# Attention of a one-core transformer step: keys on partitions, probabilities as the stationary operand, a ones column for the denominators

## What is computed

```python
def block_attention(q, k, v):
    ...
    def one_block(qblk):
        s = jnp.einsum('bkgqd,bskd->bkgqs', qblk, k).astype(jnp.float32) * scale
        p = jax.nn.softmax(s, axis=-1).astype(v.dtype)
        return jnp.einsum('bkgqs,bskd->bkgqd', p, v)
```

## Time and profile before

| | us |
|---|---|
| median of 3 runs | 3546.38 (3546.01 to 3548.62) |
| the profiled execution | 3547.59 |
| its span in the profile | 3545.8 |
| attention, from its first to its last DMA issue | 705.6 to 1744.7 |
| TensorE busy, whole span | 3171.3 (89%) |

### The profile page before, as it was taken

How to read it: one execution, slowest core, us unless ns; L and a number is a source line. 1 busy time by engine, 2 the same in 40 slices (tenths; PEclk the granted TensorE clock), 3 DMA queues, 4 the chain that set the end, 5 groups by cost and what they waited for, 6 DMA issues and landing times. The chain is left out here.

```text
span 3545.8 us, 60756 instructions
## 1 busy us (share of the span) xinstructions
PE 3171.3 (89%) x21856; PEld 2900.2 (82%) x21856; DVE 1878.6 (53%) x3485; ACT 1671.7 (47%) x3239; POOL 388.6 (11%) x400
## 2 busy tenths in 40 slices
PE   6999994759999999999699756999999999999991
PEld 6788883748888888888588645999999999999991
DVE  2222226548888888888533365545455445545443
ACT  2222220547777777777434202455455544455442
POOL 0333333500000000000000000010010000110001
PEclk9999997869999999999799855999999999999996
DMA  5121113410000000000244204565565555665545
GB/s 217 43 80 60 67 66 116 140 42 25 27 27 27 27 27 27 27 27 27 81 147 150 83 0 132 174 192 185 179 198 184 183 187 179 188 193 181 181 130 220
DMA packets 307599, 393.69 MB, mean 111 GB/s; under 512 B 13808, under 2 KB 263872, under 8 KB 306496
## 3 DMA queue, kind: packets, MB, share of 16 engines
q1 hardware_dynamic: 293680, 338.64, 28.9%
q0 software_dynamic: 10240, 35.66, 4.4%
q10 hardware_dynamic: 3600, 18.35, 1.3%
HBM read 318.68 MB, written 74.06 MB: 111 GB/s over the span
## 5 line engine op out<-in xcount | busy, mean ns | idle before, releaser
L2304 DVE TENSOR_TENSOR e_w_lo<-e_raw,e_w_hi 128x2048 fp32r<-128x2048 f32 x192 | 440.1, 2292 | 490.4 <-ACT e_w_hi L2246 490.4
L92 PE MATMUL e_ps<-e_x_hi,e_w_hi 128*128 128x272 f32 x2048 | 602.1, 294 | 5.5 <-issue 5.5
L94 PE MATMUL e_ps<-e_x_hi,e_w_lo 128*128 128x272 f32 x2048 | 593.8, 290 | 0.0
L93 PE MATMUL e_ps<-e_x_lo,e_w_hi 128*128 128x272 f32 x2048 | 590.1, 288 | 0.0
L2246 ACT ACTIVATE e_w_hi<-e_raw 128x2048 fp32r<-128x2048 f32 x192 | 366.1, 1907 | 163.7 <-DMA e_raw<-in_w_gate 159.3
L1470 DVE TENSOR_TENSOR a_pT_lo<-a_ps_t,a_pT_hi 128x512 fp32r<-128x512 f32 (+1 forms) x648 | 368.0, 601 | 139.5 <-ACT a_pT_hi L1368 139.2
L1368 ACT ACTIVATE a_pT_hi<-a_ps_t 128x512 fp32r<-128x512 f32 (+1 forms) x648 | 319.6, 532 | 185.1 <-PE a_ps_t L1238 180.5
L92 PEld LDWEIGHTS e_ps<-e_x_hi,e_w_hi 128*128 128x128 f32 x2048 | 386.1, 189 | 7.1 <-issue 5.5
L93 PEld LDWEIGHTS e_ps<-e_x_lo,e_w_hi 128*128 128x128 f32 x2048 | 386.9, 189 | 0.0
L94 PEld LDWEIGHTS e_ps<-e_x_hi,e_w_lo 128*128 128x128 f32 x2048 | 385.8, 188 | 0.0
L1443 DVE TENSOR_REDUCE a_mx<-a_ps_s 128x1 f32<-128x896 f32 (+2 forms) x392 | 346.1, 890 | 26.8 <-PE a_ps_s L1228 26.8
(11 more groups left out here) (269 smaller groups left out, 5478.2 us busy)
## 6 DMA issues: line engine op xcount, KB each, us to landing
e_raw<-in_w_gate SPq DMA_DIRECT2D x64, 1024.0 KB, 5.2
e_raw<-in_w_up SPq DMA_DIRECT2D x64, 1024.0 KB, 5.2
e_raw<-in_w_down SPq DMA_DIRECT2D x64, 1024.0 KB, 5.2
a_wm<-in_w_mod SPq DMA_DIRECT2D x32, 512.0 KB, 4.0
s_ret<-p_pr SPq DMA_DIRECT2D x17, 768.0 KB, 3.6
m_raw<-in_w_in ACTq DMA_DIRECT2D x8, 1152.0 KB, 7.1
o_cT<-s_ct SPq DMA_DIRECT2D x17, 512.0 KB, 4.7
s_x<-o_x SPq DMA_DIRECT2D x17, 512.0 KB, 4.9
```

What stands on the lines that cost most here:

```text
L92: nc.tensor.matmul(out, w_hi, x_hi, start=first, stop=False)
L93: nc.tensor.matmul(out, w_hi, x_lo, start=False, stop=False)
L94: return nc.tensor.matmul(out, w_lo, x_hi, start=False, stop=last)
L2304: nc.vector.tensor_tensor(w_lo[n % RING][:, :, :], raw[n % RING][:, :, :], w_hi[n % RING][:, :, :].bitcast(F32), ALU.subtract).then_inc(w_ ...
```

## The change

The key tile moves to the partitions of the scores. A slot is one query tile `i` and one key head `v`, thus 4 query heads side by side, 512 columns (`QCOLS`).

- Scores (L1249, L1250): a key tile is stationary, 512 query columns move; a second matmul adds the low key part. The softmax's maximum must be subtracted by matmul now, since queries are no longer on partitions: row 64 of `a_keys_lo` holds ones and row 64 of `a_qM` the negated maxima. The exponential (L1389) leaves probabilities that are transposed already.
- The maxima come from rough scores (L1222, L1218), high key part only, computed one slot ahead in the old layout: 17 pieces, 16 of 512 columns and one of four times 128, through two banks `a_ps_r`. DVE reduces each (L1496, L1493), takes the maximum of all (L1507), TensorE transposes it (L1231), ACT stores it negated.
- High and low parts are made from SBUF, two key tiles (1024 columns) at a time: `high` (ACT, L1401), `low` (DVE, L1514), 9 pairs per slot, the last with one tile.
- Value product (L1265, L1267): probabilities are stationary, per key tile and head one matmul with the high part against [ones, value high, value low], 130 columns, and one with the low part against [ones, value high], 66 columns. Column 0 of the result is the denominator, so the sums of the exponential, their reduction and the folding matmuls go. ACT copies the result out (L1410), DVE takes the reciprocal (L1530), POOL adds the halves and divides.
- The key pass keeps tile i-1 after it has rounded tile i. The load of the first queries goes ahead of it.
- Each engine walks `slot`, with 9 steps `j`; TensorE multiplies values two steps behind the scores.

```diff
+PAIRS = (KEY_TILES + 1) // 2
+QCOLS = QPK * P
+PARTS = (KEY_TILES - 1) * P // QCOLS
+PIECES = PARTS * QPK + 1
+PIECES_IN = [2, 2, 2, 2, 2, 2, 2, 3, 0]
+ONES = 2
+VCOLS = ONES + 2 * HD
+QUADS = NKV * NT
+RING = 3
...
-        prob = [k.sb(f"a_prob{i}", [P, KEY_TILES * P]) for i in range(2)]
-        pT_hi = [k.sb(f"a_pT_hi{i}", [P, KEY_TILES, GROUP, P], F32R) for i in range(2)]
-        pT_lo = [k.sb(f"a_pT_lo{i}", [P, KEY_TILES, GROUP, P], F32R) for i in range(2)]
...
+        prob = k.sb("a_prob", [P, RING, 2, QCOLS])
+        p_hi = k.sb("a_p_hi", [P, PAIRS, 2, QCOLS], F32R)
+        p_lo = k.sb("a_p_lo", [P, PAIRS, 2, QCOLS], F32R)
+        o_all = k.sb("a_o_all", [P, QPK, VCOLS])
...
+        ps_m = k.ps("a_ps_m", [P, QCOLS])
+        ps_r = [k.ps(f"a_ps_r{i}", [P, 512]) for i in range(2)]
+        ps_s = [k.ps(f"a_ps_s{i}", [P, QCOLS]) for i in range(3)]
+        ps_o = [k.ps(f"a_ps_o{i}", [P, 512]) for i in range(2)]
...
+            def combine(i, v):
+                n = quad(i, v)
+                pool.wait_ge(o_kept, 2 * n + 2)
+                nc.gpsimd.tensor_tensor(o_sum[:, :, :], o_all[:, :, ONES:ONES + HD], o_all[:, :, ONES + HD:VCOLS], ALU.add).then_inc(added, 1)
+                pool.wait_ge(added, n + 1)
+                pool.wait_ge(rsum_ok, n + 1)
+                nc.gpsimd.tensor_tensor(att[:, QPK * v:QPK * (v + 1), :], o_sum[:, :, :], spread(rsum[:, :], [P, QPK, HD]),
+                                        ALU.mult).then_inc(att_ok, 1)
...
+            def rough(i, v, n):
+                if n == 0:
+                    pe.wait_ge(emptied, use_of_queries(i, v) + 1)
+                if not (first_slot(i, v) and n < 2):
+                    pe.wait_ge(max_ok, piece(i, v, n) - 1)
+                to = ps_r[piece_bank(i, v, n)]
+                if rest_of_keys(i, n):
+                    src = (CTX_KEYS if ctx_tile(i) else KEY_TILES - 1) * P
+                    for c in range(QPK):
+                        ins = nc.tensor.matmul(to[:, c * P:(c + 1) * P], qT[v][:, c * P:(c + 1) * P], keys[:, v, src:src + P],
+                                               start=True, stop=True)
+                else:
+                    c, part = n // PARTS, n % PARTS
+                    ins = nc.tensor.matmul(to[:, :], qT[v][:, c * P:(c + 1) * P], keys[:, v, part * QCOLS:(part + 1) * QCOLS],
+                                           start=True, stop=True)
+                ins.then_inc(rough_ok, 1)
+            def turn_top(i, v):
+                pe.wait_ge(top_ok, quad(i, v) + 1)
+                pe.wait_ge(emptied, use_of_top(i, v))
+                for c in range(QPK):
+                    ins = nc.tensor.transpose(ps_m[0:HD + 1, c * P:(c + 1) * P], top[:, c, :], g["ident"][:, :])
+                ins.then_inc(filled, 1)
+            def scores(i, v, j, t):
+                c = 2 * j + t
+                n = key_tile_of(i, v, c)
+                to = ps_s[bank(i, v, c)]
+                if c == 0:
+                    pe.wait_ge(emptied, use_of_top(i, v) + 1)
+                    pe.wait_ge(qM_ok, quad(i, v) + 1)
...
+                src = CTX_KEYS if ctx_tile(i) else c
+                nc.tensor.matmul(to[:, :], keys[:, v, src * P:(src + 1) * P], qT[v][:, :], start=True, stop=False)
+                nc.tensor.matmul(to[:, :], keys_lo[:, v, src * P:(src + 1) * P], qM[v][:, :], start=False, stop=True)\
+                    .then_inc(scored, 1)
+            def value(i, v, j, t):
+                n = pair(i, v, j)
+                if t == 0:
+                    pe.wait_ge(hi_ok, n + 1)
+                    pe.wait_ge(lo_ok, n + 1)
+                    if j == 0 and not first_slot(i, v):
+                        pe.wait_ge(o_kept, 2 * quad(i, v))
...
+                for c in range(QPK):
+                    q = slice(c * P, (c + 1) * P)
+                    nc.tensor.matmul(out_block(c), p_hi[:, place(i, v, j), t, q], vals[:, src, v, :],
+                                     start=first and c in (0, 3), stop=False, skip_group_check=True)
+                    ins = nc.tensor.matmul(out_block(c)[:, 0:ONES + HD], p_lo[:, place(i, v, j), t, q], vals[:, src, v, 0:ONES + HD],
+                                           start=False, stop=last, skip_group_check=True)
+                if t == tiles_of(i, j)[-1]:
                     ins.then_inc(valued, 1)
...
+            def slot(i, v):
+                last, ahead = before(i, v), following(i, v)
+                at = 0
+                for j in range(PAIRS):
+                    todo = list(range(at, min(at + PIECES_IN[j], pieces_of(ahead[0]))))
+                    at = at + PIECES_IN[j]
+                    if j == 0:
+                        if not first_slot(i, v):
+                            for t in range(2):
+                                value(*last, PAIRS - 2, t)
+                        turn_queries(*ahead)
+                    for t in tiles_of(i, j):
+                        scores(i, v, j, t)
+                        if todo and j and t == 0:
+                            rough(*ahead, todo.pop(0))
+                    if j == PAIRS - 1:
+                        turn_top(*ahead)
+                    if j == 1 and not first_slot(i, v):
+                        value(*last, PAIRS - 1, 0)
+                    for t in range(2):
+                        if j >= 2:
+                            value(i, v, j - 2, t)
+                        if todo:
+                            rough(*ahead, todo.pop(0))
+                    if j == 2:
+                        modulation(i, v)
+                    if j == 5 and not first_slot(i, v):
+                        turn_out(*last)
...
+            def keep_keys(i, j):
                 act.wait_ge(k_turned, i + 1)
-                out = keys[:, :, :, i * P:(i + 1) * P] if isinstance(i, int) else keys[:, :, :, bass.ds(i * P, P)]
-                nc.scalar.activation(out.rearrange("p n v t -> p (n v) t"), ps_t[j][:, :, :], ACT.Copy).then_inc(k_kept, 1)
-            over_pairs(act, key_tile, 2, NTA // 2, 0)
+                at = slice(i * P, (i + 1) * P) if isinstance(i, int) else bass.ds(i * P, P)
+                nc.scalar.activation(keys[:, :, at], ps_s[j][:, 0:2 * P].rearrange("p (v t) -> p v t", t=P), ACT.Copy)\
+                    .then_inc(k_kept, 1)
+                nc.scalar.activation(keys_lo[0:HD, :, at], ps_s[j][0:HD, 2 * P:4 * P].rearrange("p (v t) -> p v t", t=P),
+                                     ACT.Copy).then_inc(k_kept, 1)
+            def key_tile(h, off):
+                round_keys(h, off)
+                if not known(h, off, 0):
+                    keep_keys(2 * h + off - 1, (off - 1) % 2)
...
+            def exps(i, v, j, t):
+                c = 2 * j + t
+                act.wait_ge(scored, key_tile_of(i, v, c) + 1)
+                if t == 0 and not (first_slot(i, v) and j < RING):
+                    act.wait_ge(lo_ok, PAIRS * (QUADS - 1) + 7 + v if ctx_tile(i) else pair(i, v, j) - RING + 1)
+                nc.scalar.activation(prob[:, place(i, v, j) % RING, t, :], ps_s[bank(i, v, c)][:, :], ACT.Exp, scale=scale)\
+                    .then_inc(exped, 1)
+            def high(i, v, j):
+                n = pair(i, v, j)
+                m = len(tiles_of(i, j))
+                act.wait_ge(exped, key_tile_of(i, v, 2 * j) + m)
...
+                nc.scalar.activation(p_hi[:, place(i, v, j), 0:m, :], prob[:, place(i, v, j) % RING, 0:m, :], ACT.Copy)\
+                    .then_inc(hi_ok, 1)
+            def keep_sums(i, v):
+                act.wait_ge(valued, pair(i, v, 0) + (1 if ctx_tile(i) else PAIRS))
+                if not first_slot(i, v):
+                    act.wait_ge(att_ok, quad(i, v))
+                for b, lo, hi in ((0, 0, 3), (1, 3, QPK)):
+                    nc.scalar.activation(o_all[:, lo:hi, :], ps_o[b][:, 0:(hi - lo) * VCOLS].rearrange("p (h f) -> p h f", f=VCOLS),
+                                         ACT.Copy).then_inc(o_kept, 1)
...
+            def slot(i, v):
+                last, ahead = before(i, v), following(i, v)
+                for j in range(PAIRS):
+                    if j == 0:
+                        keep_queries(*ahead)
+                    if j == 2 and not first_slot(i, v):
+                        keep_sums(*last)
+                    if j == 6 and not first_slot(i, v):
+                        keep_out(*last)
+                    for t in tiles_of(i, j):
+                        exps(i, v, j, t)
+                    if j == PAIRS - 1:
+                        keep_top(*ahead)
+                    high(i, v, j)
+                    if j == 2 and v == 0:
+                        queries_hi(i + 1)
...
+            def copy_queries(i, v):
+                dve.wait_ge(emptied, use_of_queries(i, v) + 1)
+                nc.vector.tensor_copy(qM[v][0:HD, :], qT[v][0:HD, :].bitcast(F32)).then_inc(qM_ok, 1)
+            def maxima(i, v, n):
+                dve.wait_ge(rough_ok, piece(i, v, n) + 1)
+                src = ps_r[piece_bank(i, v, n)]
```

(37 more changed lines are left out.)

608 lines of the change are left out of this document (235 added, 373 removed).

## The result

The changed kernel takes 4243.21 us (median of 4, 4241.84 to 4249.41), the kernel before 3547.2 on the same chip: ratio 1.197, 95% interval 1.194 to 1.199. It is slower, as forecast, but by 696 us and not by 45, far outside the range.

What follows compares the result with a forecast made beforehand. TensorE was taken as the bound: 32 slots of 32.1 us from 755 us, with corrections at the first and last, reach 1776; with the context tile 1790 against 1744.7. That is +45 on 3547.6: 3593 us, range 3520 to 3662.

Steps and rivals of the forecast that it cites:

- Price of a matmul: TensorE in attention: each narrow value product with new weights costs 0.112 us, whether 130 or 66 columns.
- that rival: Value products in attention: narrow matmuls cheaper, 0.085 us each, saving 117 us, so 3476 us; chance 5%.
- Together 30.0, so 60.0 for a tile: TensorE's work in attention: 30.0 us a slot, 60.0 a query tile, against 53.5 before.
- plus 2 for its half clock: First attention slot: 2 us added because TensorE runs it at half clock.
- 32.1: Each attention slot: 30.0 us of TensorE work plus 2.1 us of waits.
- Waits: TensorE, each slot: 1.37 us at its end, 0.23 for rough(2), 0.51 for the last slot's sums; together 2.1.
- The hand-over: Between engines, such as DVE's subtraction to TensorE's transposes: 0.03 to 0.05 us each.
- Key pass: Before the attention slots: 1.8 us a key tile against 2.87, keys ready at 741 us instead of 760.
- the 14 us for the start: Between key pass and first scores: query transposes, 17 pieces at DVE's 0.59, maxima, transposes; scores start at 755 us.
- Sign: Whole kernel: slower than before, given 76%; faster 18%, within 0.2% 6%.
- the wait at the slot's end: Step 7 to 8: value(6) waits 1.37 us for DVE's low(6), queued behind the last pieces and the maximum of all.

Runs made afterwards that it cites:

- the first row of plain matmuls: Changed kernel plus plain matmuls on TensorE alone behind attention's context tile (512 columns, pairs of 130 and 66, 130 alone, 256, two mixes); 4652.28 us, one run.
- the second row: Changed kernel plus plain matmuls behind attention's last tile: slot-like steps of 512s and pairs of 130 and 66, run behind 512s, 2-column matmuls or pairs; 4894.85 us, one run.

## Why the prediction was wrong

- **Price of a matmul: right.** 0.11 us for a product of 130 or 66 columns at the full clock, as in the earlier trace rows; 60.0 us of work for a tile, measured 60.5 where nothing waits. The Trainium skill, page "TensorE: Matmul & The Clock Gate", section "Back-to-back issue gap", has about 81 ns for each pair of a weight load and a 128-column matmul; the traces here disagree, the 130-column products alone ran 0.112 apart (2593 to 2626 us of the first row of plain matmuls), so that rival was rightly small.
- **The clock: the step that failed.** "Together 30.0, so 60.0 for a tile" was priced by rows at the full clock only, and the prediction carried this clock of the old stage over to a new mix, with "plus 2 for its half clock" as the only exception. The order put two stretches poor in wide matmuls into every slot; at a granted 0.57 the work of 30.0 us takes 30.0/0.57 = 53, measured 51.8. 32 x (51.8 - 32.1) = 630 of the missing 650 us. The rows of before could not have told: at 0.50 in the key pass and 0.63 in the context tile TensorE was also idle for much of the time (busy for 21.9 of 59.0 and 19.3 of 28.0 us). That a stage can be busy throughout and slow is new here: 277.8 of 280 us busy at 0.57. The Trainium skill, page "TensorE: Matmul & The Clock Gate", section "What's actually happening", says that activity releases the throttle; if activity is read as busy time, this trace disagrees. Neither the range nor a rival of the prediction allowed for a half clock.
- **Waits.** In the changed kernel nearly gone, since ScalarE and VectorE keep their pace while TensorE is slow (0.21 us before the transposes of the maxima at 1527.06, TensorE idle for 2.2 of 280 us). At the full clock, with the 256-column products, 1.16, 0 and 0.21 against 1.37, 0.23 and 0.51: 0.7 a slot too much, 24 us. The hand-over that the prediction put at 0.03 to 0.05 us is 0.06 in the row it names, which changes none of this.
- **Key pass: right, the start behind it too short.** The key tiles were rounded 1.83 us apart (708.1 to 739.2 us, 17 periods), forecast 1.8. First scores came at 761.3 us, forecast 755, before 764.2: of the 14 us for the start, the 16 first pieces were counted at VectorE's 0.59 each, but at the half clock TensorE set their pace, 0.79 (743.95 to 756.57).
- **Sign: luck.** Slower for the reason given would have been an estimated 3590 us (3550 without the wait at the slot's end, and 32 x 1.2) to 3620 (3653 with 256 columns, less 35 for the width); the sign of the real result was right by another mechanism.

Still open: what property of a matmul counts, and how the mix around a burst enters. Width and memory together go far: 130 columns alone held the full clock in the row and did not raise it from half, and low products of 130 gave 0.65 with the burst in place, 0.89 without it. But 130 with 66 fell in the row where 130 alone did not. And a burst can bring the clock down in wide surroundings too (nine times in the kernel before with 128 and 128, twice and three times in the two kernels with 512 columns of probabilities moving), where it is back 3.4 us later and not 41 to 48; in the kernel before and among products of 256 there was no such fall. Why some bursts do it and others don't is not shown.

## What to carry to other kernels

Before pricing a new mix of matmuls at the full clock, look for stretches of a few us without wide ones, and spread these (transposes, 2-column products, narrow value products) between wide matmuls; reordering left every count and width as it was and was worth 696 us here. Such an order keeps a full clock; it need not bring one: the steps of the second row, at the full clock for 58 us, stayed at half for 111 us behind a burst. Read the clock beside the busy time: 100% busy at 0.57 is a stage at half speed. Where 512 columns can move and the small operand can stand, that form kept the clock at 0.99 even with the burst in one row, and here also had less work.

## What the runs showed of the hardware

- The clock has a memory: the same row of matmuls stays at 2.4 GHz (58.8 us) or at 1.2 GHz (111.1 us), by what ran ahead of it.
- 16 matmuls of 2 columns, 1.8 us at the full clock, can bring it down though TensorE never pauses. How long it stays down depends on what follows: 3.4 us with 128 to 448 or with 512 columns moving, 41 to 48 us in the changed kernel, all of the 111 us of the plain steps.
- What keeps the full clock need not bring it back: behind pairs of 130 and 66, 200 products of 130 columns stayed at half, and 200 of 256 were back at the full clock for all but 1.9 us (0.96 from 3027 to 3051 us).
- At half the clock a product of 130 or 66 columns with its weights costs 0.213 us (a row of 330), at full 0.112; the weight load alone lasts 333 ns against 192, so it slows with the clock, too.
